# A chain of mixer blocks in fp32: two norms by square root and VectorE's reciprocal, and the attention bias masked by VectorE

## The chip, the core and the metric

The kernel runs as one program on one core of a Trainium2 chip. The metric is the time of one execution on the device in microseconds; the median of the runs of the kernel before is 2003.73 us (three runs, 2003.56 to 2004.02). All data and all arithmetic are fp32; a matrix product by a weight is made of three TensorE products of fp32r parts, as told below.

## What is computed

The reference is a chain of two model blocks over 256 tokens of width 1024. The first has three branches (a gated linear recurrence, an attention over neighbours and an attention over a memory), then a convolutional feed-forward. The second has two layers, with two gated feed-forwards each, an RWKV-7 time mix in the first, a chunked gated MLP in the second, and an attention over a memory in both. The three places that the change touches are these, cut from the reference:

```python
def neighbourhood_attention(zq, zk, zv, rpb, w_o):
    ...
    s = jnp.einsum('brqhd,brkwhd->bhrqkw', q, k).astype(jnp.float32) + bias.astype(jnp.float32)
    s = jnp.where(col_mask[:, None, :], s, MASK_NEG)
    p = jax.nn.softmax(s.reshape(b, NA_HEADS, rows, GRID_W, kh * GRID_W), axis=-1)
...
def rwkv7_time_mix(h, mu, w_rkv, ...):
    ...
    var = jnp.mean(jnp.square(y - mean), axis=-1, keepdims=True)
    y = ((y - mean) * lax.rsqrt(var + GN_EPS)).reshape(B, S, C)
    y = y * ln_w.astype(jnp.float32) + ln_b.astype(jnp.float32)
    y = (y + bonus.reshape(B, S, C)).astype(h.dtype)
    return (y * g) @ w_o
...
    return rms_norm(x, final_norm)
```

Here `rms_norm(x, g)` is x * rsqrt(mean(x * x) + 1e-6) * g.

## The kernel before

**Layout.** Activations are feature-major: 128 partitions by 8 x 256 columns, one "page" of 128x2048. The five engines run hand-written programs that meet through named counting semaphores, and each engine works strictly in the order of its program. `Link` (`link(...)` on VectorE) makes the engine wait for the end of its own instruction, where the next one reads the result.

**The weight stream.** All weights are one stream of blocks of 128x2048, which the SP queue loads into two raw buffers (`load_program`, L262). Each block has two halves of 1024 columns. ScalarE copies a half to a rounded high part (`high`, L1365), VectorE subtracts it from the raw half to get the low part (`low`, L2033), and TensorE makes three products of high and low parts (L308, or L372 and L375 in the feed-forwards). Four slots of a high and a low half each hold two blocks. A raw buffer is loaded again when the block in it has its low halves. `lows(seg, first, n)` is VectorE's work for n blocks, two ahead of the block that TensorE takes.

**The early stretch.** While TensorE projects the first norm by the blocks of `w_in`, VectorE's program alternates `lows` with the recurrence's gates: `forget(d)` (L2223; eight scalings of 128x256 and a maximum over 128x2048) and `keys(d)` (L2233; eight of 128x256). In the same stretch the SP queue loads the attention's position bias by 32 small transfers into pages 14 and 15, between weight blocks; the first 16 count on `bias_in`, the rest on `bias_rest`. GpSimd waits for each half, adds the column mask (0 inside the window, -1e30 outside) in eight adds of 128x256 (L2876), and counts on `bias_ready`; VectorE waits for 2 of these in the attention's first step, near 150 us.

**The group norm.** At the end of the time mix TensorE leaves the centred outputs in four banks of PSUM. ScalarE squares them in quarters of 512 columns (L1907, `rw_sq`); TensorE sums them over each head by a product with ones (L984, `rw_var`); ScalarE makes the inverse root as exp(-0.5 ln(v + eps)), first four Ln by `log_root` (L1397, `rw_varsb`), then four Exp (L1915, `rw_std`). A dummy Ln of one column at L1904 brings the table load forward. VectorE meanwhile prepares the bonus, gate, gain and bias (L2713, L2719). Then, a quarter at a time, `normed(q)` multiplies by the inverse root (L2727) and adds the bonus (L2728, `rw_out`); ScalarE rounds the quarter to its high part (`operand_high`, L1377) and VectorE makes its low part (`operand_quarter`, L2056), on which TensorE waits at every second 256 columns of the first block of `rw_o` (`operand_part`). `normed(q)` comes ahead of the low part of quarter q - 1.

**The last norm.** After the last feed-forward VectorE adds the four residual quarters (L2133), ScalarE squares them (L2012), VectorE adds pairs (L2856), TensorE sums over features (L1105), ScalarE makes Ln (L1397) and Exp (L1404) of 128x256 in `norm_root("fin2")`, VectorE scales (L2077, eight of 128x256) and the SP queue stores.

Of the kernel before, what the change touches and what calls it, by code (L numbers as in the profile page):

```python
# [26 lines left out]
ALU = mybir.AluOpType  # L27
ACT = mybir.ActivationFunctionType
AX = mybir.AxisListType.X

P = 128
D = 1024
KT = D // P
T = 256
# [88 lines left out]
hg_o hg_sq hg_var hg_varsb hg_std hg_out merged lora_mid lora_out rw_mix rw_kk2 rw_kksum rw_kkfloor  # L123
rw_kkln rw_kkvar rw_kkn rw_bonus_in rw_bonus_sum rw_bonus_sb rw_cum rw_exp rw_dec rw_t rw_t_sb rw_lx rw_mb rw_rk rw_lt rw_lx_read rw_xx
rw_plain rw_masked rw_lm rw_y rw_y_sb rw_z rw_z_sb rw_rhs0 rw_rhs1 rw_rhs_sb0 rw_rhs_sb1 rw_u0 rw_u1 rw_u_sb0 rw_u_sb1 rw_centre
rw_ds0 rw_ds1 rw_s0 rw_s1 rw_turn rw_yt rw_sq rw_var rw_varsb
rw_std rw_out fin_gain fin_log fin_inv fin_log2 fin_logs fin_std gm_vnorm gm_vstd gm_vout0 gm_vout1 gm_mask gm_mix gm_mixed gm_root gm_up
""".split()

# [1220 lines left out]
def scalar_program(act, a, t, s):  # L1350
# [44 lines left out]
    def log_root(dst, src, scale, col, var_read):  # L1395

        f(dst, src, ACT.Ln, scale=scale, bias=t.stat[:, col:col + 1]).then_inc(s[var_read], 1)  # L1397
# [371 lines left out]
    def swiglu(fi, seg, prev=None):  # L1769
        def gate(st, tile, k, first):  # L1770
            act.wait_ge(s["gate_scaled"], st + ((fi - 1) * FIT + 1))
            gate_ = t.work[:, 1024 + k * 512:1536 + k * 512]
            f(gate_, gate_, ACT.Silu).then_inc(s["gate_ready"], 1)  # L1773

        ffn(fi, seg, gate, lambda st, tile, k, first: hidden_high(fi, st, k), prev)
# [121 lines left out]
    for n_ in range(NCH):  # L1897
# [3 lines left out]
          ACT.Copy, scale=-1.0).then_inc(s["rw_rhs_sb1"], 1)  # L1901
        act.wait_ge(s["rw_u1"], n_ + 1)
        f(t.page[4][po, b * D + 512:(b + 1) * D], ps[po, 5, :], ACT.Copy).then_inc(s["rw_u_sb1"], 1)
    f(t.stat[:, 42:43], t.stat[:, COL_EPS:COL_EPS + 1], ACT.Ln)  # L1904
    act.wait_ge(s["rw_yt"], 1)
    for q in range(4):
        f(t.sq[:, q * 512:(q + 1) * 512], ps[:, q, :], ACT.Square).then_inc(s["rw_sq"], 1)  # L1907
    for q in range(4):
        c = slice(q * 512, (q + 1) * 512)
        act.wait_ge(s["rw_var"], q + 1)  # L1910
        log_root(t.page[2][:, c], ps[:, 4 + q, :], 1.0 / RW_D, COL_GN_EPS, "rw_varsb")
    for q in range(4):
        c = slice(q * 512, (q + 1) * 512)
        act.wait_ge(s["rw_varsb"], q + 1)
        f(t.page[2][:, c], t.page[2][:, c], ACT.Exp, scale=-0.5).then_inc(s["rw_std"], 1)  # L1915

    act.dma_start(t.page[5], a.bias_rows).then_inc(s["rows_in"], 16)
    act.dma_start(t.page[9], a.mix_weights).then_inc(s["rows_in"], 16)
# [87 lines left out]
    highs("gm_o", n=7)  # L2006
    memory_attention(1, BLK["gm_o"] + 7)
    swiglu(4, "ffn4", BLK["xo1"] + 3)
    for q in range(4):
        c = slice(q * 512, (q + 1) * 512)  # L2010
        act.wait_ge(s["x_up"], 4 * 4 + q + 1)
        f(t.sq[:, c], t.x[:, c], ACT.Square).then_inc(s["norm_sq"], 1)  # L2012
    norm_root("fin2")
    act.wait_ge(s["out_done"], 4 * 16)


# [1 line left out]
def vector_program(dve, t, s):  # L2018
# [214 lines left out]
    def keys(d):  # L2233

        kp = t.page[2 + d]
        for h in range(HG_H):
            c = slice(h * T, (h + 1) * T)
            ins = ts(kp[:, c], kp[:, c], t.lb[:, 16 + 8 * d + h:17 + 8 * d + h], K_FLOOR, ALU.mult, ALU.max)
        ins.then_inc(s["hg_keys"], 1)
# [10 lines left out]
    def running_keys(d):  # L2250
        dve.wait_ge(s["hg_log"], 2 * d + 2)
        dst = t.page[(7, 3)[d]]
        tt(dst, t.page[11 + d], dst, ALU.subtract).then_inc(s["hg_ready"], 1)

    forget(0)
    keys(0)
    lows("w_in", 5, 4)
    forget(1)
    keys(1)
    lows("w_in", 9, 3)  # L2260
# [459 lines left out]
                  ALU.mult, ALU.mult)  # L2720
    link(ins)

    def normed(q):

        c = slice(q * 512, (q + 1) * 512)
        dve.wait_ge(s["rw_std"], q + 1)
        link(tt(t.page[8][:, c], t.page[8][:, c], t.page[2][:, c], ALU.mult))  # L2727
        tt(t.page[7][:, c], t.page[8][:, c], t.page[0][:, c], ALU.add).then_inc(s["rw_out"], 1)  # L2728

    for q in range(4):  # L2730
        normed(q)
        if q:
            operand_quarter("rw_o", t.page[7], t.page_r[10], t.page_r[7], q - 1)
    operand_quarter("rw_o", t.page[7], t.page_r[10], t.page_r[7], 3)
    residual("rw_o", then="x0")

# [121 lines left out]

    swiglu(4, "ffn4", BLK["xo1"] + 3, after=lambda q: q and final_part(q - 1))
    final_part(3)  # L2860
    norm_scale("fin2")

def pool_program(pool, t, s):
    for col, value in ((COL_EPS, EPS), (COL_GN_EPS, GN_EPS)):
        pool.memset(t.stat[:, col:col + 1], value)
    pool.memset(t.zrow[:], 0.0).then_inc(s["zero_row"], 1)
    pool.wait_ge(s["params_in"], 16)
    pool.wait_ge(s["consts_in"], 16)  # L2870
    for page, ready in ((14, "bias_in"), (15, "bias_rest")):
        pool.wait_ge(s[ready], 16 * 2 * NA_H)
        table = t.page[page].rearrange("p (n c) -> p n c", c=NA_COLS)
        window = t.const[:, C_WINDOW:C_WINDOW + NA_COLS].unsqueeze(1).broadcast_to([P, 4, NA_COLS])
        for n in range(0, 32, 4):
            ins = pool.tensor_tensor(table[:, n:n + 4], table[:, n:n + 4], window, ALU.add)  # L2876
        ins.then_inc(s["bias_ready"], 1)
    gains, squares = par(t, "gain_fin", 0, KT), par(t, "gain_fin", KT, KT)
    pool.tensor_tensor(gains, par(t, "norm_final", 0, KT), par(t, "ffn1_norm_2", 0, KT), ALU.mult).then_inc(s["fin_gain"], 1)
    pool.tensor_tensor(squares, par(t, "norm_final", 0, KT), par(t, "norm_final", 0, KT), ALU.mult).then_inc(s["fin_gain"], 1)  # L2880
    pool.wait_ge(s["fin_gain"], 2)
    pool.wait_ge(s["hg_gh"], len(HG_STEPS) - 2)
    pool.tensor_copy(t.page[3][:, 0:KT * P].rearrange("p (k m) -> p k m", k=KT),
                     squares.unsqueeze(2).broadcast_to([P, KT, P])).then_inc(s["fin_gain"], 1)
    def wide(ap):
        return ap.rearrange("p (n j) -> p n j", j=CH)

    def mask(name):
        return folded(t, name).unsqueeze(1).broadcast_to([P, 8, CH])

    def masked(page, g, name, ready):
        pool.wait_ge(s["rw_plain"], ready)
        matrix = wide(group(page, g))
        pool.tensor_tensor(matrix, matrix, mask(name), ALU.mult).then_inc(s["rw_masked"], 1)

    for g0 in range(0, KT // 2, 2):
        done = 3 * g0
        for lv in range(len(LEVELS) - 1):
            for g in (g0, g0 + 1):
                if lv == 0:  # L2900
                    pool.wait_ge(s["rw_lt"], g + 1)
                else:
                    pool.wait_ge(s["rw_y"], inv_at(g, lv - 1) + 1)
                m = LEVELS[len(LEVELS) - 2 - lv]
                pool.tensor_tensor(wide(rw_level(t, g)), wide(rw_lower(t, g)), mask(f"upper{m}"),
                                   ALU.mult).then_inc(s["rw_lm"], 1)
            if lv == 1:
                masked(RW_M(t), g0, "strict", done + 1)
                masked(RW_RB(t), g0, "incl", done + 2)
            if lv == 2:  # L2910
                masked(RW_M(t), g0 + 1, "strict", done + 3)
                masked(RW_RB(t), g0 + 1, "incl", done + 4)
            if lv == 3:
                masked(RW_RK(t), g0, "incl", done + 5)
                masked(RW_RK(t), g0 + 1, "incl", done + 6)
# [138 lines left out]
```

## Time and profile before

| | |
|---|---|
| median of the runs | 2003.73 us |
| the profiled execution, whole | 2006.06 us |
| its span, in which all rows lie | 2004.2 us |
| TensorE busy | 1910.7 us, 95% of the span |
| VectorE busy | 1407.8 us, 70% |
| ScalarE busy | 1043.4 us, 52% |
| GpSimd busy | 60.7 us, 3% |

Rows are times from the span's start. PE is TensorE, DVE is VectorE, ACT is ScalarE, POOL is GpSimd. In a time line a row has the start, the time to the end of the last instruction of the row, the engine, line and operation, output and input, the count, and in brackets the idle time just before with what ended it.

### The profile page before, as it was taken

The page shows a single profiled execution, that of the slowest core. Times are in us where ns is not written, and L with a number is a line of the kernel's source. Part 1 is how long each engine was busy: PE and PEld are TensorE (multiplying, and loading weights), DVE is VectorE, ACT ScalarE, POOL GpSimd, SP SyncE. Part 2 cuts the span into 40 slices and gives each one's busy share as a digit, 9 for nine tenths or more (in the row PEclk, how much of TensorE's full clock was granted, in tenths as well). Part 3 has the DMA queues.
Part 4 walks back from the last instruction along what each step waited for, and adds up shares of the span by engine and source line. Part 5 has one row for each costly group of instructions (what it writes and reads, how often), then busy time and mean ns, then how long its engine had stood idle before and what let it go on. Part 6 is the DMA issues. An engine that isn't in the chain of part 4 may idle for free. (4 is left out here: it accounts for less than half of the span.)

```text
span 2004.2 us, 40742 instructions
## 1 busy us (share of the span) xinstructions
PE 1910.7 (95%) x16972; PEld 1810.0 (90%) x16972; DVE 1407.8 (70%) x1764; ACT 1043.4 (52%) x1390; POOL 60.7 (3%) x58
## 2 busy tenths in 40 slices
PE   7999997999998999999888899999999998999998
PEld 7998997999998899989888899998999998998997
DVE  6585579777777877798554657777777756557776
ACT  7565565755556444468422545445444555445443
POOL 0300000000000000000061000000000000000000
PEclk9999999999999999999999999999999999999999
DMA  6753332254553455444400334555555452534552
GB/s 230 216 187 127 127 127 106 109 207 168 188 183 133 167 190 189 169 148 148 148 4 4 147 118 177 188 189 170 188 188 189 169 189 106 189 120 175 189 189 105
DMA packets 52323, 313.50 MB, mean 156 GB/s; under 512 B 13536, under 2 KB 13792, under 8 KB 14944
## 3 DMA queue, kind: packets, MB, share of 16 engines
q1 hardware_dynamic: 51760, 308.42, 43.2%
q10 hardware_dynamic: 432, 3.15, 0.4%
q8 instruction: 105, 1.72, 0.3%
q14 instruction: 26, 0.21, 0.0%
HBM read 310.50 MB, written 1.05 MB: 155 GB/s over the span
## 5 line engine op out<-in xcount | busy, mean ns | idle before, releaser
L2033 DVE TENSOR_TENSOR wl<-raw,wh 128x1024 fp32r<-128x1024 f32 x576 | 688.9, 1225 | 376.1 <-ACT wh L1365 374.3
L1365 ACT ACTIVATE wh<-raw 128x1024 fp32r<-128x1024 f32 x575 | 586.4, 1050 | 295.2 <-PE ps L308 141.3
L308 PE MATMUL ps<-pages_r,wh 128*128 128x256 f32 x2480 | 547.4, 287 | 34.0 <-DVE wl L2033 13.8
L308 PE MATMUL ps<-pages_r,wl 128*128 128x256 f32 x1680 | 478.7, 285 | 0.0
L308 PEld LDWEIGHTS ps<-pages_r,wh 128*128 128x128 f32 x2480 | 424.4, 195 | 38.5 <-issue 16.5
L308 PE MATMUL ps<-norm_r,wh 128*128 128x256 f32 x2336 | 431.4, 285 | 6.1 <-DVE wl L2033 4.2
L308 PEld LDWEIGHTS ps<-norm_r,wh 128*128 128x128 f32 x2336 | 366.8, 192 | 9.6 <-issue 5.8
L372 PE MATMUL ps<-norm_r,wh 128*128 128x512 f32 x1408 | 355.1, 394 | 2.6 <-DVE wl L2033 1.7
L308 PE MATMUL ps<-norm_r,wl 128*128 128x256 f32 x1184 | 335.4, 283 | 0.0
L308 PEld LDWEIGHTS ps<-pages_r,wl 128*128 128x128 f32 x1680 | 326.1, 194 | 0.0
L372 PEld LDWEIGHTS ps<-norm_r,wh 128*128 128x128 f32 x1408 | 253.5, 189 | 50.4 <-DVE wl L2033 2.3
L308 PE MATMUL ps<-work_r,wh 128*128 128x256 f32 x976 | 272.1, 285 | 0.0
L308 PEld LDWEIGHTS ps<-norm_r,wl 128*128 128x128 f32 x1184 | 227.6, 192 | 0.0
L375 PEld LDWEIGHTS ps<-norm_r,wl 128*128 128x128 f32 x1408 | 192.0, 190 | 13.8
L375 PE MATMUL ps<-norm_r,wl 128*128 128x256 f32 x1408 | 196.2, 282 | 0.0
L308 PEld LDWEIGHTS ps<-work_r,wh 128*128 128x128 f32 x976 | 187.1, 194 | 0.1
L1698 ACT ACTIVATE pages_r<-work 128x512 fp32r<-128x512 f32 x55 | 34.8, 632 | 207.4 <-DVE work L2549 180.1
L1773 ACT ACTIVATE work<-work 128x512 f32<-128x512 f32 x44 | 27.8, 632 | 134.9 <-DVE work L2112 134.9
L308 PE MATMUL ps<-wh,norm_r 128*128 128x256 f32 x448 | 81.8, 285 | 0.0
L308 PEld LDWEIGHTS ps<-wh,norm_r 128*128 128x128 f32 x448 | 69.8, 192 | 1.3 <-ACT pages L1456 1.3
L2112 DVE TENSOR_TENSOR work<-work,rstd 128x512 f32<-128x512 f32 x88 | 60.5, 687 | 9.3 <-ACT rstd L1404 5.6
L2425 DVE TENSOR_TENSOR work_r<-work,pages_r 128x512 fp32r<-128x512 f32 x55 | 38.1, 692 | 38.4 <-ACT pages_r L1698 38.4
(332 smaller groups left out, 1863.9 us busy)
## 6 DMA issues: line engine op xcount, KB each, us to landing
raw<-in_stream SPq DMA_DIRECT2D x287, 1024.0 KB, 4.8
pages<-in_rpb SPq DMA_DIRECT2D x32, 64.0 KB, 6.2
pages<-in_mem SPq DMA_DIRECT2D x2, 512.0 KB, 6.1
raw<-in_stream SPq DMA_DIRECT2D x2, 512.0 KB, 7.5
x<-in_x SPq DMA_DIRECT2D x1, 1024.0 KB, 11.8
pages<-in_mem ACTq DMA_DIRECT2D x1, 1024.0 KB, 5.0
pages<-in_gmlp_b ACTq DMA_DIRECT2D x1, 1024.0 KB, 4.9
pages<-in_gmlp_w ACTq DMA_DIRECT2D x1, 1024.0 KB, 7.0
```

What stands on the lines that cost most here:

```text
L308: mm = pe.matmul(out, left, right, start=start and q == 0, stop=stop and q == 2, skip_group_check=True)
L372: mm = pe.matmul(ps[:, bank + j, :], wh[:, cols], t.norm_r[:, 2 * k * T:2 * (k + 1) * T], start=k == 0, stop=False, skip_group_check=True)
L375: mm = pe.matmul(ps[:, bank + j, T:2 * T], wl[:, cols], t.sq_r[:, k * T:(k + 1) * T], start=False, stop=k == KT - 1, skip_group_check=True)
L1365: f(t.wh[(2 * b0 + hf) % PIECE_SLOTS][:], t.raw[b0 % 2][:, hf * 1024:(hf + 1) * 1024], ACT.Copy).then_inc(s["high_done"], 1)
L1698: f(hidden_parts(t, k)[0], t.work[:, k * 512:(k + 1) * 512], ACT.Copy).then_inc(s["hidden_high"], 1)
L1773: f(gate_, gate_, ACT.Silu).then_inc(s["gate_ready"], 1)
L2033: tt(t.wl[i][:], t.raw[b0 % 2][:, hf * 1024:(hf + 1) * 1024], t.wh[i][:].bitcast(F32), ALU.subtract).then_inc(s["low_done"], 1)
L2112: return tt(out.rearrange("p (n t) -> p n t", n=n), in_, t.rstd[:, :].unsqueeze(1).broadcast_to([P, n, T]), ALU.mult)
L2425: tt(low_, t.work[:, k * 512:(k + 1) * 512], high_.bitcast(F32), ALU.subtract).then_inc(s["hidden_ready"], 1)
```

## The change

The group norm's Ln and Exp become one Sqrt on ScalarE and a reciprocal on VectorE (the same for the last norm), the dummy instruction becomes a Sqrt, one more dummy Sqrt stands ahead of the last squares, and the add of the bonus is put behind the low part of the quarter before. The mask of the position bias is added by VectorE in one instruction of 128x2048 a page, the first after `keys(0)`, the second after the four weight blocks that follow.

```diff
@@ scalar_program, group norm
-    f(t.stat[:, 42:43], t.stat[:, COL_EPS:COL_EPS + 1], ACT.Ln)
+    f(t.stat[:, 42:43], t.stat[:, COL_EPS:COL_EPS + 1], ACT.Sqrt)
...
         act.wait_ge(s["rw_var"], q + 1)
-        log_root(t.page[2][:, c], ps[:, 4 + q, :], 1.0 / RW_D, COL_GN_EPS, "rw_varsb")
-    for q in range(4):
-        c = slice(q * 512, (q + 1) * 512)
-        act.wait_ge(s["rw_varsb"], q + 1)
-        f(t.page[2][:, c], t.page[2][:, c], ACT.Exp, scale=-0.5).then_inc(s["rw_std"], 1)
+        f(t.page[2][:, c], ps[:, 4 + q, :], ACT.Sqrt, scale=1.0 / RW_D,
+          bias=t.stat[:, COL_GN_EPS:COL_GN_EPS + 1]).then_inc(s["rw_std"], 1)
@@ scalar_program, last norm
     swiglu(4, "ffn4", BLK["xo1"] + 3)
+    f(t.stat[:, 43:44], t.stat[:, COL_EPS:COL_EPS + 1], ACT.Sqrt)
...
-    norm_root("fin2")
+    act.wait_ge(s["norm_sum"], NORM["fin2"] + 1)
+    f(t.rstd[:], ps[:, 4, 0:T], ACT.Sqrt, scale=1.0 / D, bias=t.stat[:, COL_EPS:COL_EPS + 1]).then_inc(s["norm_std"], 1)
@@ vector_program, early stretch
+    def masked_bias(page, ready):
+        dve.wait_ge(s[ready], 16 * 2 * NA_H)
+        table = t.page[page].rearrange("p (n c) -> p n c", c=NA_COLS)
+        outside = t.const[:, C_WINDOW:C_WINDOW + NA_COLS].unsqueeze(1).broadcast_to([P, 32, NA_COLS])
+        tt(table, table, outside, ALU.add).then_inc(s["bias_ready"], 1)
+
     forget(0)
     keys(0)
+    masked_bias(14, "bias_in")
     lows("w_in", 5, 4)
+    masked_bias(15, "bias_rest")
     forget(1)
     keys(1)
@@ vector_program, group norm
-    def normed(q):
-
+    for q in range(4):
         c = slice(q * 512, (q + 1) * 512)
         dve.wait_ge(s["rw_std"], q + 1)
+        link(dve.reciprocal(t.page[2][:, c], t.page[2][:, c]))
         link(tt(t.page[8][:, c], t.page[8][:, c], t.page[2][:, c], ALU.mult))
-        tt(t.page[7][:, c], t.page[8][:, c], t.page[0][:, c], ALU.add).then_inc(s["rw_out"], 1)
-
-    for q in range(4):
-        normed(q)
         if q:
             operand_quarter("rw_o", t.page[7], t.page_r[10], t.page_r[7], q - 1)
+        tt(t.page[7][:, c], t.page[8][:, c], t.page[0][:, c], ALU.add).then_inc(s["rw_out"], 1)
@@ vector_program, last norm
     final_part(3)
+    dve.wait_ge(s["norm_std"], NORM["fin2"] + 1)
+    link(dve.reciprocal(t.rstd[:], t.rstd[:]))
     norm_scale("fin2")
@@ pool_program
-    for page, ready in ((14, "bias_in"), (15, "bias_rest")):
-        pool.wait_ge(s[ready], 16 * 2 * NA_H)
-        table = t.page[page].rearrange("p (n c) -> p n c", c=NA_COLS)
-        window = t.const[:, C_WINDOW:C_WINDOW + NA_COLS].unsqueeze(1).broadcast_to([P, 4, NA_COLS])
-        for n in range(0, 32, 4):
-            ins = pool.tensor_tensor(table[:, n:n + 4], table[:, n:n + 4], window, ALU.add)
-        ins.then_inc(s["bias_ready"], 1)
```

## Rows read from the trace of the kernel before

**Rows 1.** The page's part 1: busy us, share, instructions by engine.

```profile
PE 1910.7 (95%) x16972; PEld 1810.0 (90%) x16972; DVE 1407.8 (70%) x1764; ACT 1043.4 (52%) x1390; POOL 60.7 (3%) x58
```

**Rows 2.** Time line of TensorE: its two waits in the early stretch.

```profile
81.50 0.47 PE L308 MATMUL ps<-norm_r,wh 128*128 128x256 f32 x2 [2.03 <-DVE wl L2033]
...
106.26 0.47 PE L308 MATMUL ps<-norm_r,wh 128*128 128x256 f32 x2 [1.49 <-DVE wl L2033]
```

**Rows 3.** Time line of VectorE, 70 to 110 us (third row: narrower window).

```profile
70.53 2.90 DVE L2033 TENSOR_TENSOR wl<-raw,wh 128x1024 fp32r<-128x1024 f32 x2 [4.98 <-ACT wh L1365]
73.36 3.50 DVE L2228 TENSOR_SCALAR pages<-pages,lb 128x256 f32<-128x256 f32 x8
75.17 1.05 DVE L2228 TENSOR_SCALAR pages<-pages,lb 128x256 f32<-128x256 f32 x3
...
80.14 4.62 DVE L2033 TENSOR_TENSOR wl<-raw,wh 128x1024 fp32r<-128x1024 f32 x4
88.50 2.36 DVE L2033 TENSOR_TENSOR wl<-raw,wh 128x1024 fp32r<-128x1024 f32 x2 [3.74 <-ACT wh L1365]
95.16 3.02 DVE L2033 TENSOR_TENSOR wl<-raw,wh 128x1024 fp32r<-128x1024 f32 x2 [4.31 <-ACT wh L1365]
98.11 3.51 DVE L2228 TENSOR_SCALAR pages<-pages,lb 128x256 f32<-128x256 f32 x8
...
104.89 4.62 DVE L2033 TENSOR_TENSOR wl<-raw,wh 128x1024 fp32r<-128x1024 f32 x4
```

**Rows 4.** Time line of GpSimd: the adds of the mask.

```profile
67.14 7.63 POOL L2876 TENSOR_TENSOR pages<-pages,const 128x256 f32<-128x256 f32 x8 [66.13 <-DMA pages<-in_rpb]
91.91 7.62 POOL L2876 TENSOR_TENSOR pages<-pages,const 128x256 f32<-128x256 f32 x8 [17.13 <-DMA pages<-in_rpb]
```

**Rows 5.** One line's instructions, L2253: count, least/median/most ns, starts, form.

```profile
L2253 DVE TENSOR_TENSOR pages<-pages x2: 2281/2282/2283, 140.4 to 144.9; 128x2048 f32<-128x2048 f32 x2
```

**Rows 6.** Time line of ScalarE in the group norm.

```profile
1103.59 0.69 ACT L1397 ACTIVATE pages<-ps,stat 128x512 f32<-128x512 f32 x1 [0.70 <-PE ps L984]
...
1108.83 0.63 ACT L1915 ACTIVATE pages<-pages 128x512 f32<-128x512 f32 x1
```

**Rows 7.** Time line of VectorE in the group norm.

```profile
1101.52 3.23 DVE L2719 SCALAR_TENSOR_TENSOR pages<-ps,param,pages 128x256 f32<-128x256 f32 x8 [6.80 <-ACT norm L1907]
1109.56 0.69 DVE L2727 TENSOR_TENSOR pages<-pages 128x512 f32<-128x512 f32 x1 [4.81 <-ACT pages L1915]
1110.29 0.69 DVE L2728 TENSOR_TENSOR pages<-pages 128x512 f32<-128x512 f32 x1
1110.90 0.68 DVE L2727 TENSOR_TENSOR pages<-pages 128x512 f32<-128x512 f32 x1
```

**Rows 8.** TensorE's restart; two stretches: busy us by engine, PEclk, DMA share, GB/s.

```profile
1113.06 0.76 PE L308 MATMUL ps<-pages_r,wh 128*128 128x256 f32 x2 [6.26 <-DVE pages_r L2056]
...
1113.00:1118.20 5.20, 5.14 (x24) 5.18 (x25) 4.39 (x7) 1.26 (x2) 0.00 (x0) 0.50 0.46 192
1118.40:1125.00 6.60, 6.60 (x57) 6.60 (x57) 3.05 (x3) 2.74 (x3) 0.00 (x0) 1.00 0.04 5
```

**Rows 9.** Two lines' instructions on VectorE, small tiles.

```profile
L2171 DVE RECIPROCAL stat<-stat x12: 155/158/166, 152.7 to 243.1; 128x2 f32<-128x2 f32 x12
L2201 DVE RECIPROCAL lb<-lb x1: 246/246/246, 20.1 to 20.1; 128x16 f32<-128x16 f32 x1
```

**Rows 10.** Time lines of TensorE, ScalarE and VectorE at the end.

```profile
1992.99 2.45 PE L1105 MATMUL ps<-work,const 128*128 128x256 f32 x8
...
1994.25 1.28 ACT L1397 ACT_TABLE_LOAD   x1
1995.54 0.47 ACT L1397 ACTIVATE rstd<-ps,stat 128x256 f32<-128x256 f32 x1
1996.03 1.28 ACT L1404 ACT_TABLE_LOAD   x1
...
1997.78 3.26 DVE L2077 SCALAR_TENSOR_TENSOR norm<-x,param,rstd 128x256 f32<-128x256 f32 x8 [3.09 <-ACT rstd L1404]
```

More of the change, by code:

```diff
@@ L125 @@
 rw_plain rw_masked rw_lm rw_y rw_y_sb rw_z rw_z_sb rw_rhs0 rw_rhs1 rw_rhs_sb0 rw_rhs_sb1 rw_u0 rw_u1 rw_u_sb0 rw_u_sb1 rw_centre
-rw_ds0 rw_ds1 rw_s0 rw_s1 rw_turn rw_yt rw_sq rw_var rw_varsb
+rw_ds0 rw_ds1 rw_s0 rw_s1 rw_turn rw_yt rw_sq rw_var
 rw_std rw_out fin_gain fin_log fin_inv fin_log2 fin_logs fin_std gm_vnorm gm_vstd gm_vout0 gm_vout1 gm_mask gm_mix gm_mixed gm_root gm_up
```

## The prediction, made before the change was timed

> **What bounds the kernel now.** I read the engine shares first, then, for each place that the change touches, the time lines of TensorE, VectorE, ScalarE and GpSimd over the same microseconds. TensorE is busy for 1910.7 us of a span of 2004.2 us [rows 1], so an edit counts only where TensorE waits for the edited work, or at the very end. There are three such places.
>
> First, the early weight stretch. TensorE stands still twice, 2.03 us until 81.50 and 1.49 us until 106.26, and both times what releases it is VectorE's subtraction at L2033, the low half of a weight piece [rows 2]. VectorE works without a pause from 70.53 to the low halves at 80.14, and from 95.16 to those at 104.89: two halves, then the helper `forget`, then `keys`, then the halves that TensorE waits for [rows 3]. Anything put into either chain reaches TensorE in full. Second, the group norm: TensorE stops after the variance sums and starts again at 1113.06 after 6.26 us, released by the low part of the first operand quarter [rows 8]. Third, the tail: nothing runs beside the last norm.
>
> **Part 1, the bias masks go from GpSimd to VectorE.** Removed: two times eight GpSimd adds, 67.14 to 74.77 and 91.91 to 99.53 [rows 4]. Added: two VectorE adds of 128x2048, the first right after `keys(0)` and ahead of the low halves at 80.14, the second right after the pair at 95.16 and ahead of `forget(1)`. The nearest row is the add of 128x2048 at L2253, 2.28 us [rows 5]; one starts about 0.08 us before the one ahead of it has ended, so each pushes its successors by 2.20 us. Both are ahead of low halves for which TensorE already waits, so the cost is 2 x 2.20 = 4.4 us before what is given back.
>
> What is given back: VectorE is slower where GpSimd works. A pair of low halves takes 2.36 us at 88.50 but 2.90 at 70.53 and 3.02 at 95.16 [rows 3]: 0.54 and 0.66 us. `forget`'s eight instructions take 3.50 and 3.51 us; three of them after GpSimd's end take 1.05 [rows 3], so about 0.32 from start to start and 2.64 for eight: 0.86 us each. All of this stands in the same two chains. First chain: +2.20 - 0.54 - 0.86 = +0.80. Second: +2.20 - 0.66 - 0.86 = +0.68. They add up, since the second begins with a weight block whose load is released by a low half of the first. TensorE leaves this stretch **1.5 us later**; the ends are +4.4 (nothing given back) and -2.9 (the adds wholly hidden), and I take the rows' own sum.
>
> New waits: VectorE now waits for the bias tables itself, with the weight halves queued behind it. GpSimd, which had nothing else to do, started at 67.14 and 91.91 upon their landing [rows 4]; VectorE comes to its adds at about 78.8 and 98. The slack is 11 and 6 us, so these waits cost nothing; from a landing 6 us later they would.
>
> **Part 2, the group norm.** Removed from ScalarE: four Exp of about 0.6 us, the first at 1108.83, and a table load of 1.28 us ahead of them [rows 6, 10]. Four Ln (0.69 us each, the first at 1103.59) become four Sqrt of the same shape [rows 6]; I take the same time for them. The first result stands at 1104.28 instead of 1109.46 and the last by 1107.5, where the table load began (1108.83 less 1.28). Added on VectorE: four reciprocals of 128x512, each with a wait for its own end, ahead of the multiply.
>
> What does one cost? The trace has no large one. It has 128x2 at 158 ns (twelve of them) and 128x16 at 246 ns [rows 9]: 88 ns for 14 elements, 6.3 ns an element. An ordinary instruction of 512 columns takes 0.69 us [rows 7] and one of 2048 takes 2.28 [rows 5], 1.04 ns an element and 0.16 us fixed. So 128x512 would take 0.158 + 510 x 0.0063 = **3.37 us**, and 128x256 1.76 us. Bounds: if large ones run like ordinary work, 0.69 us; if all of the 246 ns were per element, 15.4 ns and 7.9 us. With the ordinary fixed part the slope is 5.3 ns and the cost 2.85 us; if only 0.11 were fixed, 8.3 ns and 4.4 us. I take the two reciprocals' own line, since it lies through both of them.
>
> The Trainium skill ("VectorE: DVE Perf Modes", section "First, the fixed hardware budget") says that reciprocal is an iterative divide with a repeat count of 8. If that is read as eight of that page's 0.96 GHz cycles an element, an estimate is 4.3 us for 512 elements and a total some 4 us above mine; the two small rows show a slope of about six cycles instead.
>
> Now the order on VectorE, where the change also moves the add of a quarter behind the low part of the quarter before. It is free at 1104.75 [rows 7], with the first Sqrt done. A linked instruction pushes the next by its time plus 0.04, an unlinked one by 0.61: the reciprocal by 3.40, the multiply by 0.73, the low part by 0.61 and the add by 0.61 (starts in rows 7). Quarter 0: reciprocal 1104.78, multiply 1108.18, add 1108.91. Quarter 1: reciprocal 1109.52, multiply 1112.92, low part of quarter 0 1113.65, add 1114.26. Each further quarter takes 5.35: the low part of quarter 1 at 1119.00, of 2 at 1124.35, of 3 at 1126.3 (add to 1125.65, ScalarE's high part to 1126.30). ScalarE is ready in time for each. TensorE can begin quarter 0 at about 1114.4, 1 at 1119.8, 2 at 1125.2, 3 at 1127.1.
>
> A quarter is 12 matmuls. TensorE's clock was granted at 0.50 (1.2 GHz) over 1113.0 to 1118.2 after the idle stretch, with 24 matmuls in 5.2 us (0.213 each), and at 1.00 (2.4 GHz) from 1118.4, 57 matmuls in 6.60 with both edges counted (0.12 each) [rows 8]. Before, matmul 24 began at 1113.06 + 24 x 0.213 = 1118.17. After, quarters 0 and 1 are short bursts between waits, and I take it that the low clock again covers some 25 matmuls from the last restart, at 1125.2: shift 1125.2 - 1118.17 = 7.0, and 25 x (0.213 - 0.12) = 2.3 for matmuls that ran at full clock before. **+9.3 us**. At full clock from that restart quarter 3's start binds: 1127.15 against 1119.7, +7.5. Each 0.1 us of reciprocal moves this by 0.4. Afterwards weights are prepared in step with TensorE as before, so nothing takes it back.
>
> **Part 3, the last norm.** Before: Ln's table load from 1994.25, Ln 1995.54 to 1996.01, Exp's table load, Exp, first scaling at 1997.78 [rows 10]. After: Sqrt's table load lies in ScalarE's idle time before the last residual; Sqrt waits for the last sum, whose matmuls end at about 1995.44 [rows 10]; + 0.47, reciprocal 1.76, two hand-overs of 0.04: first scaling at about 1997.75. Two table loads and an Exp leave, a reciprocal enters: **-0.0 us** (0.3 less if the sum's modelled end is late, -1.3 with a reciprocal of ordinary price).
>
> Ln and Exp each have a load of 1.28 us with the instruction 0.01 to 0.02 us behind it [rows 10]. The Trainium skill ("ScalarE: Activation LUTs", section "What ACT_TABLE_LOAD costs") adds a drain of about 1.38 us to each switch: by that the tail would shed some 2.7 us more; the rows show no such time, so I leave it out.
>
> **Sum.** +1.5 + 9.3 - 0.0 = +10.8 us. The profiled execution took 2006.06 us, 1.86 beyond its span and 2.3 above the median of 2003.73; the shifts are differences, so they go on the median: **2014.5 us**.
>
> **Rivals.** (a) The reciprocal is steeper, 4.4 us: 4 x 1.03 = 4.1 more, and 0.5 more in the tail, 2019.1. For it: two tiny sizes fix a slope badly. Against: it puts the fixed part well below the 0.16 of ordinary work. Chance 0.13. (b) A large reciprocal streams like any instruction, 0.69 us. Then VectorE's round is 2.67 us a quarter; the first low part is held by ScalarE's fourth Sqrt (to 1107.5) and high part, so until about 1108.25 and TensorE restarts at 1109.1: -3.9; tail -1.3; masks +1.5; 2000.0, not slower. It decides below about 1.3 us each (2.2 ns an element). Against: the 246 ns row. Chance 0.07. (c) The masks' give-back doesn't come, as VectorE waits there for something else: +2.8, 2017.3. Chance 0.08. (d) The masks cost nothing, since weights' landing absorbs them: 2013.0. For it: the pair at 95.16 waited 4.31 us for ScalarE's high half [rows 3]. Against: that half hangs on a load released by VectorE itself. Chance 0.10. (e) The low clock doesn't come back in the last burst, 2012.7: 0.12. The forecast has 0.50.
>
> **How the numbers follow.** The forecast with (c), (d) and (e) spans 2011 to 2018; (a) reaches 2019.1; a shallower slope of 5.3 ns gives 2.1 + 0.3 less, 2012.1. The range of 2010.5 to 2019.5 leaves out (b) and combinations such as (a) with (c). A measurement tells about 0.2%, 4 us, from no change: slower needs a reciprocal above some 1.7 us. Slower 0.92, within 0.05, faster 0.03: (b) lies on the border between the last two.
>
> **What would show it.** Reciprocals of 128x512 at L2730 or so near 3.4 us and of 128x256 near 1.8; the three gaps of TensorE in the first block after the group norm, each 2.6 to 3 us; TensorE's waits near 82 and 108 longer by 0.8 and 0.7; pairs of low halves at 2.36 throughout; an equal tail. I am wrong if a large reciprocal costs as much as a multiply, or if the masks stop TensorE for a table that hasn't landed.

## The result, and the profile after

| | before | after |
|---|---|---|
| median of the runs | 2004.02 us (5) | 2017.76 us (5, 2014.69 to 2020.75) |
| the profiled execution, whole | 2006.06 us | 2017.30 us |
| its span | 2004.2 us | 2015.5 us |

The ratio is 1.0056 with a 95% interval of 1.0042 to 1.0071, or +11.2 us (+8.4 to +14.2); the medians lie 13.7 us apart and the two profiled spans 11.3. The forecast was 2014.5 us (+10.8), with a range of 2010.5 to 2019.5.

All reciprocals of the changed kernel, from the groups of instructions by line with shapes kept apart (count | busy us, mean ns of one | idle before):

```profile
L2733 DVE RECIPROCAL pages<-pages 128x512 f32<-128x512 f32 x4 | 13.4, 3348 | 0.0
...
L2866 DVE RECIPROCAL rstd<-rstd 128x256 f32<-128x256 f32 x1 | 1.8, 1753 | 1.3 <-ACT rstd L2012 1.3
...
L2200 DVE RECIPROCAL lb<-lb 128x16 f32<-128x16 f32 x1 | 0.2, 244 | 0.0
```

The large tiles lie on the line of the two small ones of [rows 9]: (3348 - 1753) / 256 = 6.2 ns an element.

TensorE's waits in the early stretch and in the group norm (time line of TensorE, rows with idle time ahead of them), which answer to [rows 2] and [rows 8]:

```profile
83.62 0.48 PE L308 MATMUL ps<-norm_r,wh 128*128 128x256 f32 x2 [3.84 <-DVE wl L2032]
...
109.37 0.47 PE L308 MATMUL ps<-norm_r,wh 128*128 128x256 f32 x2 [0.99 <-DVE wl L2032]
...
1104.66 5.40 PE L984 MATMUL ps<-norm,const 128*128 128x512 f32 x8 [0.70 <-ACT norm L1907]
1117.63 0.77 PE L308 MATMUL ps<-pages_r,wh 128*128 128x256 f32 x2 [7.58 <-DVE pages_r L2055]
...
1122.86 0.80 PE L308 MATMUL ps<-pages_r,wh 128*128 128x256 f32 x2 [2.33 <-DVE pages_r L2055]
...
1128.27 0.77 PE L308 MATMUL ps<-pages_r,wh 128*128 128x256 f32 x2 [2.47 <-DVE pages_r L2055]
```

TensorE leaves the early stretch 3.1 us later (109.37 against 106.26), and in the group norm it now waits three times, for the low parts of quarters 0, 1 and 2. VectorE in the early stretch, against [rows 3]:

```profile
71.82 2.36 DVE L2032 TENSOR_TENSOR wl<-raw,wh 128x1024 fp32r<-128x1024 f32 x2 [5.65 <-ACT wh L1365]
74.10 2.67 DVE L2227 TENSOR_SCALAR pages<-pages,lb 128x256 f32<-128x256 f32 x8
...
80.05 2.28 DVE L2258 TENSOR_TENSOR pages<-pages,const 128x2048 f32<-128x2048 f32 x1
82.25 4.62 DVE L2032 TENSOR_TENSOR wl<-raw,wh 128x1024 fp32r<-128x1024 f32 x4
...
97.58 2.36 DVE L2032 TENSOR_TENSOR wl<-raw,wh 128x1024 fp32r<-128x1024 f32 x2 [4.12 <-ACT wh L1365]
99.85 2.29 DVE L2258 TENSOR_TENSOR pages<-pages,const 128x2048 f32<-128x2048 f32 x1
102.05 2.67 DVE L2227 TENSOR_SCALAR pages<-pages,lb 128x256 f32<-128x256 f32 x8
...
108.00 4.62 DVE L2032 TENSOR_TENSOR wl<-raw,wh 128x1024 fp32r<-128x1024 f32 x4
```

The mask costs 2.28 us, the pair of low halves is back at 2.36 and `forget`'s eight at 2.67. From the pair to the low halves that TensorE wants, the first chain takes 82.25 - 71.82 = 10.43 us against 9.61 before, the second 108.00 - 97.58 = 10.42 against 9.73. But the first chain also begins 1.29 us later than before, ahead of the first mask.

VectorE in the group norm, against [rows 7]: one round of the chain.

```profile
1112.69 3.35 DVE L2733 RECIPROCAL pages<-pages 128x512 f32<-128x512 f32 x1
1116.07 0.69 DVE L2734 TENSOR_TENSOR pages<-pages 128x512 f32<-128x512 f32 x1
1116.80 0.69 DVE L2055 TENSOR_TENSOR pages_r<-pages,pages_r 128x512 fp32r<-128x512 f32 x1
1117.41 0.68 DVE L2737 TENSOR_TENSOR pages<-pages 128x512 f32<-128x512 f32 x1
1118.01 3.35 DVE L2733 RECIPROCAL pages<-pages 128x512 f32<-128x512 f32 x1
```

A quarter takes 1118.01 - 1112.69 = 5.32 us. The clock there (stretches; us, busy and count by engine, PEclk, DMA share, GB/s):

```profile
1117.60:1120.30 2.70, 2.67 (x12) 2.63 (x12) 2.70 (x2) 0.63 (x1) 0.00 (x0) 0.50 0.02 6
...
1128.20:1131.90 3.70, 3.63 (x17) 3.66 (x18) 2.44 (x3) 1.58 (x2) 0.00 (x0) 0.50 0.00 0
1131.90:1134.00 2.10, 2.10 (x19) 2.10 (x19) 0.00 (x0) 0.94 (x1) 0.00 (x0) 0.97 0.00 0
```

The low clock covers all three bursts and 17 matmuls after the last restart. The end, against [rows 10]:

```profile
1997.72 1.28 ACT L2006 ACT_TABLE_LOAD   x1
...
2007.14 0.47 ACT L2012 ACTIVATE rstd<-ps,stat 128x256 f32<-128x256 f32 x1 [1.25 <-PE ps L1105]
...
2007.64 1.75 DVE L2866 RECIPROCAL rstd<-rstd 128x256 f32<-128x256 f32 x1 [1.30 <-ACT rstd L2012]
2009.43 3.26 DVE L2076 SCALAR_TENSOR_TENSOR norm<-x,param,rstd 128x256 f32<-128x256 f32 x8
```

The first scaling comes 2009.43 - 1997.78 = 11.65 us later than before, and the first sum of the last norm (L1105) 11.6 us later: up to the first scaling the tail gives and takes nothing.

### The profile page after: what moved, and what is told of

It reads as the page before. It is cut to its first block and busy times, and to the rows that moved or that the text cites. A ratio compares the mean times of both kernels' runs of the same rounds, so it can differ in the third digit from the quotient of the medians.

```text
span 2015.5 us, 40726 instructions
## 1 busy us (share of the span) xinstructions
PE 1914.5 (95%) x16967; PEld 1813.7 (90%) x16972; DVE 1425.2 (71%) x1771; ACT 1038.3 (52%) x1384; POOL 45.4 (2%) x42
## 5 line engine op out<-in xcount | busy, mean ns | idle before, releaser
L375 PEld LDWEIGHTS ps<-norm_r,wl 128*128 128x128 f32 x1408 | 192.0, 190 | 13.8
## 6 DMA issues: line engine op xcount, KB each, us to landing
x<-in_x SPq DMA_DIRECT2D x1, 1024.0 KB, 11.9
```

Source lines behind the costliest of these rows:

```text
L375: mm = pe.matmul(ps[:, bank + j, T:2 * T], wl[:, cols], t.sq_r[:, k * T:(k + 1) * T], start=False, stop=k == KT - 1, skip_group_check=True)
```

## Marks for comparing thirteen traces

One execution differs from the next by several microseconds, so I cut each trace at four instructions of TensorE: the attention's first product (L508), the start of the group norm's variance sums (L984), the first product of the memory's heads (L998) and the first sum of the last norm (L1105). Their first starts are below, in us (lines are 6 higher in the two kernels with filler). The last column is what I call the stage: the group norm and the product behind it. A restart is TensorE's first matmul after a wait in it.

```
                   L508     L984     L998    L1105   L998-L984
before            147.6   1101.5   1156.7   1993.0     55.2
after             150.8   1104.7   1168.3   2004.6     63.6
e1_group_norm     148.8   1113.0   1177.4   2013.8     64.4
e2_masks          150.6   1107.1   1159.6   1995.9     52.5
e3_masks_late     146.5   1103.4   1156.8   1993.2     53.4
e5_gn_multiply    148.2   1104.8   1156.6   1992.8     51.8
e6_masks_both     155.7   1109.8   1162.6   1998.8     52.8
e7_gn_one_root    148.5   1102.6   1152.0   1988.4     49.4
e8_best           147.3   1102.2   1151.6   1987.9     49.4
e9_fill           149.8   1105.8   1169.3   2005.7     63.5
e10_add_first     149.1   1103.7   1168.7   2005.1     65.0
e11_fill_three    147.9   1103.2   1166.6   2003.0     63.4
e12_before_again  146.9   1100.4   1155.8   1992.1     55.4
```

From L998 to L1105 every trace takes 836.2 to 836.4 us. From L508 to L984, where nothing is edited, they take 953.5 (the kernel before, again) to 964.2 (e1): this is what moves the totals from run to run.

## The experiments

The ratios below are against runs of the kernel before on the same chip, whose medians were 2007.25 us (29 runs, with e1, e2, e3 and e6) and 2005.57 (23 runs, with e5, e7, e8 and e9); a ratio is turned into us by 2004, and the numbers in brackets are its 95% interval. e10, e11 and e12 have one execution each and are read from their traces alone.

**The two parts one by one.** e1 has only the group norm's edits, e2 only the masks' edits, each as in the diff of the change.

> The group norm's part of the change alone (Sqrt, reciprocal of 128x512, the add behind the low part); masks and last norm as before. My theory: the shift of the group norm in the full change is four reciprocals of 3.35 us in one chain on VectorE, so this alone gives +8.5 us (2012 to 2013), with the early stretch as before: TensorE's two waits of about 2.0 and 1.5 us, and three waits in the first block after the group norm of about 7.6, 2.3 and 2.5 us. Rival: part of the loss comes from the early stretch reaching further, then this alone gives less than +7 us.

> The masks' part alone, VectorE adding them at the change's places. My theory: the chains on VectorE grow by 0.80 and 0.68 us, so TensorE leaves the stretch 1.5 us later; the 3.2 us seen in the trace of the changed kernel hold 1.3 + 0.3 us of weight blocks that landed later by chance, ahead of the first mask, and come and go between executions. Expected +1.5 us, and from the start of the low halves of the tenth block to the low halves behind the first mask 10.4 us, as in the changed kernel. Rival: the landing is later because of the change (GpSimd's absence or VectorE's reads shift the transfers): then +3.2 us again, with the tenth block's low halves again at 71.8 and not 70.5.

Measured: e1 1.0050 (1.0031 to 1.0069), +10.0 us; e2 1.0005 (0.9990 to 1.0020), +1.0 us (-2 to +4). Together +11.0, the change's +11.2. e1's own trace is an unlucky one (span 2025.0, of which 6.5 us were lost against e12's trace in 17 us at half clock in the scan ahead of the norm, 1087.6 to 1104.6), but its restarts in the norm are the changed kernel's: waits of 9.27, 2.33 and 2.48 us, at the same distances (13.0, 18.2 and 23.6 us after L984). So the rival, that the norm's loss came from the early stretch, falls. In e2 the tenth block's pair began at 70.80 and not 71.82 or later, while in e1, with the masks on GpSimd, it began at 72.49. So the late landing isn't the change's doing: it comes and goes. From that pair to the low halves behind the mask e2 took 81.23 - 70.80 = 10.43 us, as expected. Over the five traces with the masks at the change's places (after, e2, e9, e10, e11) L508 lies at 147.9 to 150.8, mean 149.6; over the five with the masks on GpSimd (before, e1, e5, e7, e12) at 146.9 to 148.8, mean 148.0: **+1.6 us**, where the sum had 1.5. The five scatter by about a microsecond, so this mean is known to about 1.4 us either way; the chains' own rows are the sharper evidence.

e1 also shows that what GpSimd costs VectorE is a matter of timing. Its tables landed at 67.21 and its adds were nearly over when VectorE came:

```profile
67.21 5.59 POOL L2870 TENSOR_TENSOR pages<-pages,const 128x256 f32<-128x256 f32 x8 [66.20 <-DMA pages<-in_rpb]
...
72.49 2.53 DVE L2030 TENSOR_TENSOR wl<-raw,wh 128x1024 fp32r<-128x1024 f32 x2 [5.98 <-ACT wh L1365]
74.94 2.66 DVE L2225 TENSOR_SCALAR pages<-pages,lb 128x256 f32<-128x256 f32 x8
```

2.53 and 2.66 us, not 2.90 and 3.50: there the first chain had next to nothing to give back (0.17 us).

**The masks where VectorE is idle.**

```diff
-    lows("w_in", 9, 3)
+    lows("w_in", 9, 2)
+    masked_bias(14, "bias_in")
+    lows("w_in", 11, 1)
+    masked_bias(15, "bias_rest")
```

> The masks added by VectorE, but each ahead of a low half that waits for a landing anyway: the first after two more weight blocks and the second after a third, near 110 and 115 us, where VectorE sat idle for 3.6 and 4.1 us. My theory: the adds of 2.2 us vanish in the idle time and VectorE keeps what GpSimd's absence gives back, 1.40 and 1.52 us, so TensorE leaves the stretch 2.9 us earlier than before: -2.9 us. Rival: the stretch hangs on the landing of weights and not on VectorE: then 0, and e2 also 0. Second rival: a mask costs by its reads and not by its place: then the same as e2.

Measured: 0.9976 (0.9965 to 0.9988), -4.8 us (-7.0 to -2.4), which holds the -2.9. Neither of TensorE's two waits is left in this trace; the first wait for a low half is at 129.07 (e8, with the same masks, still has one of 1.95 us at 82.29). With the same two instructions of 2.28 us the kernel is 1.0 us slower when they stand in front of a low half and 4.8 us faster when they stand behind it. The place decides: the two intervals just don't overlap. L508 lies at 146.5 here and 147.3 in e8, 1.1 us ahead of the mean with GpSimd, which is less than the total's interval asks for. In this trace the stage, which e3 doesn't edit, is also some 1.9 us shorter than in the two traces of the kernel before (53.4 against 55.2 and 55.4); the rest is not located.

**GpSimd beside VectorE.** The edit adds GpSimd's sixteen adds again, from the constants into pages 13 and 8, and the attention waits for 4 on `bias_ready`.

```diff
+        source = t.const[:, 0:T].rearrange("p (n c) -> p n c", c=NA_COLS)
+        table = t.page[(13, 8)[page - 14]].rearrange("p (n c) -> p n c", c=NA_COLS)
...
+            ins = pool.tensor_tensor(table[:, n:n + 4], source, window, ALU.add)
```

> As e2, but GpSimd also makes its sixteen adds at its old times, of a constant table into two pages not in use (left aside). It brings back GpSimd's presence beside VectorE without its dependence. My theory: two instructions of two SBUF inputs, one on each engine, hold each other up, so the pairs of low halves at 70 and 95 us take 2.9 to 3.0 us again and the eight scalings 3.5 us: +2.9 over e2, so +4.4 against before. Rival: those long instructions had another cause (the tables' transfers landing): then the same as e2 with or without GpSimd.

Measured: 1.0032 (1.0016 to 1.0047), +6.4 us, 5.4 more than e2. VectorE's rows:

```profile
72.65 3.26 DVE L2033 TENSOR_TENSOR wl<-raw,wh 128x1024 fp32r<-128x1024 f32 x2 [2.18 <-ACT wh L1365]
75.84 3.94 DVE L2228 TENSOR_SCALAR pages<-pages,lb 128x256 f32<-128x256 f32 x8
...
100.83 2.90 DVE L2033 TENSOR_TENSOR wl<-raw,wh 128x1024 fp32r<-128x1024 f32 x2 [3.25 <-ACT wh L1365]
103.66 2.83 DVE L2259 TENSOR_TENSOR pages<-pages,const 128x2048 f32<-128x2048 f32 x1
106.41 3.09 DVE L2228 TENSOR_SCALAR pages<-pages,lb 128x256 f32<-128x256 f32 x8
```

Over 2.36, 2.67, 2.36, 2.29 and 2.67 this is 0.90 + 1.27 + 0.54 + 0.54 + 0.42 = 3.7 us more. So GpSimd's work itself stretches VectorE's, and the give-back is real. GpSimd is held up in turn: its two sets of adds last 8.76 and 9.94 us. VectorE's loss was under-expected by 0.8, since its own mask now met GpSimd too. The other 1.4 us of this trace's L508 (155.7 against 150.6) fit a later landing (the tenth block's pair begins at 72.65, not 70.80), which no run isolates.

**The reciprocal replaced by a multiply**, in e1's kernel. It leaves out the inverse, so its output isn't the norm; its time is what counts:

```diff
-        link(dve.reciprocal(t.page[2][:, c], t.page[2][:, c]))
+        link(tt(t.page[2][:, c], t.page[2][:, c], t.page[2][:, c], ALU.mult))
```

> The group norm's part alone, as in e1, but each reciprocal of 128x512 is replaced by an ordinary multiply of the tile with itself (the inverse is left out). Everything else, with its order and its waits for its own end, stays. This is the price of my rival (b). My theory: the whole loss is the reciprocal's own 3.35 us against 0.69; TensorE restarts about 3.9 us earlier than before the change, held by ScalarE's fourth root and its high part, and the total is -3.9 us against before, 14 below e1. Rival: the added instruction, its waits and the other order cost something whatever the operation: then the total is not below before.

Measured: 0.9992 (0.9983 to 1.0002), -1.6 us (-3.4 to +0.4), 11.6 below e1. The stage takes 51.8 us instead of 64.4. The reciprocals' own difference is 4 x (3.35 - 0.69) = 10.6 us, so nearly the whole loss is the operation; the added instruction, its waits and the order cost nothing that shows. The restart came 7.65 us after the sums began. The theory had ScalarE's fourth root hold it, but here that root had ended at 4.4 us, and VectorE worked without a pause from its preparation to the low part: VectorE held it. Against the old stage the gain is smaller than my price of rival (b), for a reason that e12 bears on below.

**The moved add.** The changed kernel with the add of a quarter ahead of the low part of the one before:

```diff
+        tt(t.page[7][:, c], t.page[8][:, c], t.page[0][:, c], ALU.add).then_inc(s["rw_out"], 1)
         if q:
             operand_quarter("rw_o", t.page[7], t.page_r[10], t.page_r[7], q - 1)
-        tt(t.page[7][:, c], t.page[8][:, c], t.page[0][:, c], ALU.add).then_inc(s["rw_out"], 1)
```

> The full change, with the add of a quarter ahead of the low part of the quarter before, as the kernel before had it. It prices the moved line. My theory: each restart of TensorE comes 0.6 us later (13.6 instead of 13.0 us after the variance sums begin, and so on), the last low part 0.6 us earlier; as the third quarter's twelve matmuls take longer than this, the first block ends 0.3 to 0.6 us later. The move was right and small. Rival: the order matters more, since ScalarE's high part of a quarter hides behind it: then the stage is shorter by up to 2 us with the add first.

Measured in one trace: restarts 13.6, 18.8 and 24.2 us after L984, each 0.6 later than in the change, and 65.0 us for the stage against 63.6 and 64.4. The direction is as expected. The clock stayed at 0.50 until 1133.48 there, for 26 matmuls after the last restart; e1, with 25, is the trace to compare with: 65.0 - 64.4 = 0.6 us, all of it in the restart, the upper end of what was expected.

**The clock.** The changed kernel with idle matmuls in TensorE's waits:

```diff
+        if name == "rw_o" and k % 2 == 0:
+            if k == 0:
+                pe.wait_ge(s["rw_std"], 4)
+            for _ in range(20 if k == 0 else 7):
+                pe.matmul(ps[:, 7, :], t.zrow[:, :], t.zrow[:, 0:1].broadcast_to([P, 512]), ...)
```

> The full change, with idle matmuls of TensorE in the waits of the group norm (20 ahead of the first quarter, once the four roots are made, and 7 ahead of each other quarter, of zeros into a bank not in use; they add nothing to the result). It takes away the half clock as a cause. My theory: of the group norm's shift about 2 us are the clock (the quarters and the first matmuls after the last restart at 1.2 GHz), the rest is VectorE's chain, which the filler can't shorten: the restarts stay at the same distance from each other, the clock is granted at 1.0 throughout, and the change loses 2 us less: +9 instead of +11 against before. Rival: the clock's price is larger, since the whole stage hangs on it: then 4 us or more come back.

Measured: 1.0073 (1.0050 to 1.0096), +14.6 us and not the +9 expected, with 63.5 us for the stage: nothing won. The first restart, 3.79 us after the last filler, was again at half clock. From 1124.0 on the clock was granted at 1.0, but the restarts lay at 12.9, 18.2 and 23.5 us after the sums, as in the change, and the seven fillers ahead of the last quarter held TensorE from 1130.86 to 1132.21, while that quarter's low part ended at 1131.26. e11 leaves those out: `(20, 7, 7, 0)[k // 2]`.

> e9 without the idle matmuls ahead of the last quarter, where they stood in its way (the third quarter ended about 1.5 us ahead of the fillers' end, and the fourth was ready 0.9 us before that). It gives the clock's price in the group norm. My theory: from the start of the variance sums to the first product of the memory's heads 62.6 us instead of 63.6: the clock costs the change 1.0 us there, and not the 2.3 us that I put in the prediction. Rival: again 63.5 us, so that the clock costs nothing and VectorE's chain alone sets the end; or 61 us, the prediction's term.

Measured in one trace: 63.4 us. But without them the clock fell again in the last burst:

```profile
1120.00:1123.00 3.00, 2.50 (x17) 1.76 (x16) 2.97 (x4) 0.63 (x1) 0.00 (x0) 1.00 0.00 0
1123.00:1126.00 3.00, 1.63 (x8) 0.54 (x7) 2.93 (x3) 0.00 (x0) 0.00 (x0) 1.00 0.00 0
1126.00:1129.00 3.00, 2.29 (x11) 2.29 (x12) 2.05 (x4) 1.58 (x2) 0.00 (x0) 0.64 0.00 0
1129.00:1132.00 3.00, 3.00 (x22) 3.00 (x22) 1.13 (x1) 0.61 (x1) 0.00 (x0) 0.79 0.02 5
```

So neither filler isolates the clock's price. But the traces do, side by side. From the last restart on, all kernels with the same norm run the same instructions, and they differ in how many matmuls follow each other by 0.21 us and not 0.12 (my count, from the starts). The clock behind the last restart in e1 and in e2, against the rows above of the change:

```profile
1136.64:1142.16 5.52, 5.52 (x26) 5.52 (x27) 2.37 (x3) 1.60 (x3) 0.00 (x0) 0.50 0.00 0
...
1117.05:1120.01 2.96, 2.96 (x14) 2.96 (x15) 2.89 (x5) 0.63 (x1) 0.00 (x0) 0.50 0.71 293
```

The window of e1 counts one matmul more than begins slowly, and so does that of e2. All nine:

```
                   matmuls at half clock    last restart to L998
new norm
after                      17                    40.0
e1_group_norm              25                    40.8
e10_add_first              26                    40.8
e11_fill_three             16                    39.9
old norm
before                     25                    43.6
e12_before_again           26                    43.7
e3_masks_late              23                    43.4
e6_masks_both              17                    42.9
e2_masks                   13                    42.6
```

Each matmul at half clock costs its 0.09 us in full, in either norm. So the fillers won nothing for another reason than e11's rival has it, that the clock costs nothing: e11 had 16 such matmuls behind its last restart, about as many as the change. e9 had none there (39.9 us), but its own fillers let the last quarter's first matmul start 2.89 us after the restart, where the change starts it after 2.70, and the quarter began with a gap of its own; this took back most of the 0.46 us that its five remaining matmuls gained. What a full clock would win in the change is an estimate: 17 matmuls at 0.09 are 1.6 us, of which some 0.5 would have gone into waiting for the last low part (done at 1130.11).

**The kernel before, once more.**

> The kernel before, once more, for its trace. My theory: the stretch of the group norm (start of the variance sums to the first product of the memory's heads) was long by chance in the trace from which I predicted, 55.2 us, because the clock was granted at one half both in the variance sums and for 5.3 us after the restart; in the three experiments with the old group norm it took 52.5 to 53.4. So 52.5 to 53.5 us again here, with TensorE's restart about 10.0 us after the sums begin instead of 11.6. Rival: the old group norm of the whole kernel before always takes 55 us, and the masks' edits shortened it.

Here my theory fell. The stage took 55.4 us, as in the first trace, and TensorE restarted 1112.07 - 1100.41 = 11.66 us after the sums began. In both traces of the kernel before, and in that of the change, the clock was granted at one half within the variance sums; in the ten others it was not, and the eight matmuls spread over 3.1 us instead of 4.8. Which of these a run gets, and why the traces of e2, e3 and e6 with the old norm all got the fast one, I can't tell from one trace each: the rival, that the masks' edits shorten the old norm, is not excluded, though the change has the same masks and got the slow one. The old stage then has two lengths:

```profile
1100.41 5.40 PE L984 MATMUL ps<-norm,const 128*128 128x512 f32 x8 [0.70 <-ACT norm L1907]
1112.07 0.77 PE L308 MATMUL ps<-pages_r,wh 128*128 128x256 f32 x2 [6.26 <-DVE pages_r L2056]
```

and in e2, with the clock at 1.0 in the sums:

```profile
1107.09 3.70 PE L984 MATMUL ps<-norm,const 128*128 128x512 f32 x8 [0.70 <-ACT norm L1907]
1117.05 0.77 PE L308 MATMUL ps<-pages_r,wh 128*128 128x256 f32 x2 [6.26 <-DVE pages_r L2056]
```

11.66 and 9.96 us to the restart: the old norm hangs on the last sum, by way of ScalarE's table load and Exp. The new one restarts 12.9 to 13.0 us after L984 in every trace with the change's order, since VectorE starts its first reciprocal before the last sum is done. So the change costs 8 to 9 us in the stage when the sums are slow and 10 to 12 when they are fast (64.4 - 52.5 = 11.9 at most). The spread within each is the count of matmuls at half clock, as in the table above: 11.9 sets 25 of them against 13. With 25 on both sides and slow sums in the old norm it is 64.4 - 55.2 = 9.2 us.

**A root without a reciprocal, and the whole.** e7 is e1 with one function for the inverse root on ScalarE; e8 adds e3's masks and the same function in the last norm.

```diff
-        f(t.page[2][:, c], ps[:, 4 + q, :], ACT.Sqrt, scale=1.0 / RW_D,
+        f(t.page[2][:, c], ps[:, 4 + q, :], ACT.Abs_reciprocal_sqrt, scale=1.0 / RW_D,
           bias=t.stat[:, COL_GN_EPS:COL_GN_EPS + 1]).then_inc(s["rw_std"], 1)
...
-        link(dve.reciprocal(t.page[2][:, c], t.page[2][:, c]))
```

> The group norm alone, with ScalarE's function for the reciprocal square root of the absolute value in place of Sqrt and no instruction on VectorE for the inverse. My theory: ScalarE's chain is the bound in either case, so TensorE restarts 4.0 us earlier than before the change, as in e5 or 0.1 us better: -4.1 us. Rival: the function is slower than Sqrt or needs a table load between the squares and itself: then 1.3 to 3 us of it are lost and -1 to -3 us are left.

> e7's group norm, the last norm by the same function without a reciprocal, and the masks late as in e3. My theory: the three places are in series on TensorE or behind it, so their gains add: -4.1 (group norm), -2.9 from the rows or -4.8 as e3 was measured (masks), -1.8 (last norm: two table loads, an Exp and no reciprocal): -9 to -11 us against before. Rival: a part is given back by a later wait for weights: then less than -6 us.

Measured: e7 0.9981 (0.9968 to 0.9994), -3.8 us; e8 **0.9944 (0.9932 to 0.9957), -11.2 us**, median 1995.62: faster than both kernels. The stage takes 49.4 us in both, with a restart 6.3 us after the sums began. That is 1.3 us ahead of e5, where the theory had 0.1 at most: VectorE's chain, shorter by the multiply, still held it. The function takes 0.69 us for 128x512, as Sqrt and Ln do, with no table load between the squares and it:

```profile
1101.99 2.06 ACT L1907 ACTIVATE norm<-ps 128x512 f32<-128x512 f32 x4 [6.59 <-PE ps L927]
...
1105.52 0.69 ACT L1911 ACTIVATE pages<-ps,stat 128x512 f32<-128x512 f32 x1 [0.17 <-PE ps L984]
```

The gains add within the intervals (-3.8, -4.8 and a forecast -1.8 make -10.4), as the three places are in series; the tail from L1105 to the end took 9.1 us and not 11.2. With e1 this also separates ScalarE's side from VectorE's: the shorter root wins 3.8 us, the reciprocal with its root then loses 13.8.

## Why the prediction was right, point by point

- **What bounds**: right. TensorE's waits at L2033 and at the restart were the places; from L998 on nothing moved (836.3 us in both).
- **The reciprocal**: 3.37 and 1.76 us forecast, 3.348 and 1.753 measured. The slope of two small tiles held over a factor of 32. Rival (a), and the reading of the Trainium skill's repeat count of 8 ("VectorE: DVE Perf Modes", "First, the fixed hardware budget") as eight cycles an element, are answered by the same row: 6.2 ns are six cycles of that page's 0.96 GHz.
- **VectorE's order**: restarts forecast 12.9, 18.3 and 23.7 us after the sums, measured 13.0, 18.2 and 23.6. The waits between the bursts were 2.33 and 2.47 us, a little under the 2.6 to 3 that I gave as a sign.
- **The clock's term**: 25 matmuls at the low clock after the last restart were assumed. The profiled execution of the change had 17, which is 1.6 us instead of 2.3, and the stage came to +8.4 instead of +9.3. e1 and e10 had 25 and 26, and e1's stage lies 9.2 us above the one that I worked from. So the price of a matmul was right; the count, which I took for a constant, differs from trace to trace (13 to 26 over both norms). It is the one term of the sum that was mis-sized in the profiled pair.
- **The masks**: +0.80 and +0.68 forecast, +0.82 and +0.69 measured in the chains; +1.6 us in the mean of five traces each. The profiled pair shows +3.2, of which 1.29 and 0.3 us stand ahead of the two chains, in weights that landed later in that execution. So the sign that I gave, waits longer by 0.8 and 0.7, failed: the first grew by 1.8 us and the second shrank by 0.5, and only the chains' own rows carry the two numbers. One step was weaker than I put it: the give-back isn't fixed, since it hangs on when the tables land (e1), so the first chain's term is +0.8 to +2.0.
- **The last norm**: 0.0 forecast, 0.0 measured. The hidden table load stood in ScalarE's idle time. The load before Ln and the one before Exp cost 1.28 us each and no drain behind them showed, so the further gain worked out from the Trainium skill ("ScalarE: Activation LUTs", "What ACT_TABLE_LOAD costs") did not come.
- **The rivals**: (b) had its price wrong. The restart itself came 7.65 us after the sums began (e5), and 1109.1 - 1101.5 = 7.6 was worked out; but VectorE's chain held it there and not ScalarE's fourth root, so that match is luck in part. And the old restart that I compared it with came after 11.6 us in the trace at hand and after 10.0 where the sums are fast. So -1.6 us was measured instead of -3.9. (c), no give-back, falls by the chains' rows (2.36 and 2.67 us in the change) and by e6; its price should have read +2.9, 4.4 less 1.5. (d), masks that cost nothing where they stand, falls by e3 against e2. The mean of 1.6 us, known to 1.4, lies between the two rivals' 0 and 2.9 and alone decides little.
- **The sum**: +10.8 against +11.2 (8.4 to 14.2). The mechanisms held, and the two parts alone gave +10.0 and +1.0 us. That the numbers lie so close is partly luck. In the profiled pair (+11.3) the early stretch was 1.7 us dearer than forecast by a late landing, the norm 0.9 cheaper by the clock, and the rest lies behind the first scaling of the tail. And the old norm has two lengths; against one with fast sums the whole norm costs up to 2.6 us more than I gave it (11.9 against 9.3), which the range held, but the prediction doesn't foresee it.

## What to carry to other kernels

A reciprocal on VectorE costs six times as much per element as an add or a multiply of two tiles there: on a tile as wide as 512 columns it takes 3.35 us where ScalarE's inverse root takes 0.69. Where TensorE waits for it, make the inverse in the root's own instruction, as e7 does, or find a narrower tile for it (not tried here). Two sizes of an operation in the trace, however small, give its slope; look for them before assuming that it streams. And an instruction's price is its place: the same 2.28 us cost TensorE time ahead of a half that it waits for, and nothing a few instructions further on.

## What the runs showed of the hardware

- The group norm's sums ran at either clock level from one kernel or run to the next (8 matmuls spread over 3.1 or 4.8 us), and a chain that hangs on them moves by 1.7 us, one that doesn't by nothing.
- A matmul of 128x256 at half clock behind the last restart of the group norm costs 0.09 us, and nothing behind it takes that back: 8 more of them made the stretch to L998 0.8 us longer (e1 against the change), 13 more 1.2 us (e12 against e2).
- After TensorE's first wait in the early stretch, of 3.84 us where it had been 2.03, the clock fell to 1.2 GHz, which it hadn't in the trace before. The wait's length alone doesn't decide it: in e5 the clock fell at the same place behind a wait of 1.90 us. In the changed kernel TensorE came to the second wait 3.6 us later (108.38 against 104.77), and that wait shrank to 0.99 us: the slow matmuls were hidden by a wait for VectorE. The row (stretch of the changed kernel, columns as above):

```profile
84.10:87.50 3.40, 3.40 (x18) 3.40 (x18) 2.78 (x3) 0.00 (x0) 0.00 (x0) 0.50 0.49 145
```

- The stretch from L508 to L984, the same in all kernels, took 953.5 to 964.2 us. The cost of one edited place can be read from marks in single traces better than from totals, but one trace doesn't tell which clock the same stretch gets in another.
